# One flow for all attention: projection jobs of one bank beside every attention iteration

## The chip, the cores and the metric

The kernel runs on one core of one Trainium2 chip. The metric is the device time in microseconds (us), here the median of three runs. The core has a matrix engine (TensorE, PE in the profile, with its weight loads as PEld), VectorE (DVE), ScalarE (ACT), GpSimd (POOL) and the queue engine SyncE (SP). PE writes into a memory of eight banks of 128 rows by 512 fp32 columns.

## The reference

Two blocks of two layers each run one after the other on 512 tokens of width 1024. What matters here is where attention stands beside projections:

```python
def first_block(x, mem, ...):                    # twice
    a_in, b_x, b_b, b_c, q, k, v, gate_in = split_cols(rmsnorm(x) @ w_in[l], IN_SPLITS)
    br_a = multiscale_pool(a_in, pool_w[l], pool_scale[l]) @ w_branch_a[l]      # windows 2, 4, 8, 16
    br_b = (b_b * causal_dwconv(b_c * b_x, conv_b_w[l])) @ w_branch_b[l]
    br_c = dilated_attention(rope(q), rope(k), v) @ w_branch_c[l]               # 12 heads of 64
    x = x + rmsnorm((gates * branches).sum() @ w_out[l])
    x = x + rmsnorm(memory_cross_attention(rmsnorm(x), rmsnorm(mem), ...))      # 4 heads of 128, 256 keys
    x = x + rmsnorm(conv_swiglu(rmsnorm(x)))
def second_block(x, c, ctx, ...):
    # layer 0 ("AB"): window attention of 8 heads, and differential attention (two softmaxes) of 4
    # layer 1 ("C"): latent attention of 16 heads, queries and keys of 96, 768 keys, values of 64
```

## The kernel before

Every product is made of three matmuls in a split format (`mm3`, L452 to L454: high by high, low by high, high by low). A weight slab is 1024 rows by 128 columns. SP loads it into a ring of four, ACT casts its high part (`head`, L429), POOL makes its low part (`tail`, L436), and PE multiplies it with 512 token columns in 24 matmuls (`slab`, L456), or in 24 more of 256 columns where the 256 context tokens (T = 768) are in it too. PE's results go to two pairs of banks, `acc[0]` and `acc[1]`; transposed probabilities go to the pair `pt`, and there are two single banks, `ob[0]` and `ob[1]`.

An attention iteration is 128 queries of one head: scores on PE into an `acc` pair; the row maximum on DVE (L919, L1145 or L1138); the exponential on ACT (L895, L1085); six transposes on PE into `pt` (L862, L1033); a copy to the memory `sq` on ACT (L902, L1096); the product with the values on PE ("pv", L868, L1058); and on DVE a reciprocal and a scaling by it, here called the result (L942, L1164), which frees the bank that pv wrote.

- First block. In each of two layers four pool slabs and nine convolution slabs come first, with their DVE work (L2086 to L2120), then the mixing of the pool groups (L2135). Then twice (j = 0, 1) nine tiles of queries, keys and values (`pe_tiles`, L717; the rotary turn is a matmul with a permutation, L728) and eight attention iterations with no projection beside them (`pe_attention`, L844). Then the branch gates. The memory attention has twelve tiles and then sixteen iterations.
- Second block. `pe_stream` (L974) runs AB and C with parts of the next projection slabs beside the iterations. All scores of one iteration are in `acc[0]` (in AB's double iterations, those of the second map in `acc[1]`), and a tile of 768 columns takes the whole of `acc[1]`. The order in an iteration is scores, transposes, transposes of values, part of a tile, pv. The pv of iteration n writes `ob[n % 2]`. In C a head is four iterations, and its jobs are a query tile of 3 row groups and a key and value tile of 2.

The engines run their own programs and meet at semaphores; `dve_stream` (L1120) has in each iteration the maxima, the result of an earlier iteration, the end of the last tile and the start of the next.

Of the kernel before, what the change touches and what calls it, by code (L numbers as in the profile page):

```python
# [20 lines left out]
ALU = mybir.AluOpType  # L21
ACT = mybir.ActivationFunctionType
F32 = mybir.dt.float32
# [34 lines left out]
MH = 4  # L58
# [7 lines left out]
N_LOADS = 25  # L66
# [6 lines left out]
class Counts:  # L73
# [4 lines left out]
    def __init__(self):  # L78
        self.here, self.outer, self.narrow = {}, {}, False
# [12 lines left out]
    def turn(self, what):  # L92

        n = self.count(what)
        return 1 + n % 2 * 2 if self.narrow else n % 4
# [18 lines left out]
def two_blocks(nc, A, out):  # L114

    with ExitStack() as ctx:
# [25 lines left out]
        perm = keep("perm", [P, P])  # L142
# [29 lines left out]
        mask1 = z("mask1", [P, RES, TC], BF16)  # L172
# [3 lines left out]
        ql = z("ql", [P, 3, SEQ], F32R)  # L176
        kh = z("kh", [P, 3, SEQ], F32R)
        kl = z("kl", [P, 3, SEQ], F32R)
        vt = z("vt", [P, 3, RES, P])
        ot1 = z("ot1", [P, RES, P])  # L180
        z = Region(qkv_at, high)
        mgh = z("mgh", [P, KT, SEQ], F32R)
        mgl = z("mgl", [P, KT, SEQ], F32R)
        z = Region(qkv_at, high)
        ub = z("ub", [P, 2, PAD + SEQ])
        sa = z("sa", [P, 2, PAD + SEQ])
        poh = z("poh", [P, 4, SEQ], F32R)
        pol = z("pol", [P, 4, SEQ], F32R)
        zc = z("zc", [P, 2, PAD + SEQ])
        bxs = z("bxs", [P, 2, SEQ])  # L190
# [10 lines left out]
        ofl = z("ofl", [P, 4, SEQ], F32R)  # L201

# [37 lines left out]
        head_t = nc.alloc_sbuf_tensor_at("head_t", [P, SEQ], F32, offset=zone + 4 * TC)  # L240
        lat = z("lat", [P, 5, TC])
# [104 lines left out]
        s_sum, s_hi, s_raw, s_vt, s_ready = sem("s_sum"), sem("s_hi"), sem("s_raw"), sem("s_vt"), sem("s_ready")  # L346
        neg_ready = sem("neg_sink")
# [267 lines left out]
        def pe_linear_y(e, c, T, xh, xl, kt, ready, ada=(), flush=False):  # L615
            kts = [(k, k, P) for k in range(kt)]

            def body(e, i):
                for j in range(2):
                    slab(e, c, T, xh, xl, kts, fresh=1 if i + j == 0 else 0, ready=ready)  # L620
# [96 lines left out]
        def pe_tiles(e, c, tiles, kts, xh, xl, fresh=0, stats=False):  # L717

            take(e, c, acc_free + ([] if stats else [pt_free]) + ob_free)

            def post(j):
                t = tiles[j]
                e.wait_ge(raw_ready, c.next(raw_ready))
                if t["kind"] == "plain":
                    return
                if t["kind"] == "rope":
                    M = t["M"]
                    e.matmul(ob[j % 2][0:M, 0:SEQ], perm[0:M, 0:M], t2raw(j)[0:M, 0:SEQ], start=True,  # L728
                             stop=True).then_inc(post_done, 1)
                else:  # L730
                    n, r0 = t["n"], t["r0"]
                    past(e, pe_past)
                    for i, cols in enumerate(t["tok"]):
                        tr = e.transpose(pt[:, i * n // 512, i * n % 512:i * n % 512 + n],
                                         t2raw(j)[r0:r0 + n, cols], ident[r0:r0 + n, r0:r0 + n])
                    tr.then_inc(post_done, 1)

            out, last_v = 0, -1
            for j in range(len(tiles) + 1):
                if fresh and j == 0:  # L740
                    pe_wave(e, c, tiles[0]["T"], xh, xl, fresh=fresh, free=False, stats=stats)
                elif j < len(tiles) and not (fresh and j == 1):
                    t = tiles[j]
                    slab(e, c, t["T"], xh, xl, t.get("kts", kts), M=t["M"], free=False, c0=t.get("c0", 0))
                if j == 2 and stats:
                    take(e, c, [pt_free])
                if j:

                    if tiles[j - 1]["kind"] in ("v", "kv"):
                        need, last_v = last_v + 1, j - 1  # L750
                        if need > out:
                            e.wait_ge(tile_ready, c.next(tile_ready, need - out))
                            out = need
                    post(j - 1)
            e.wait_ge(tile_ready, c.next(tile_ready, len(tiles) - out))
            give(e, acc_free + [pt_free] + ob_free)

        def t2raw(j):
            return sq[:, j % 2, :]

        def act_tiles(e, c, tiles):

            N, at = len(tiles), []
            for j in range(N + 2):
                if j < N:
                    head(e, c)
                    at.append(c.turn("acc"))
                    done = c.next(slab_done)
                if 1 <= j <= N:
                    t = tiles[j - 1]  # L770
                    T, M = t["T"], t["M"]
                    if not t.get("rx"):
                        e.wait_ge(slab_done, done if j == N else done - 1)
                    need = c.next(tile_ready) if j >= 3 else 0
                    if not t.get("rx"):
                        if need:
                            e.wait_ge(tile_ready, need)
                        e.activation(v3(t2raw(j - 1)[0:M, 0:T], T), bank(at[j - 1], T, M), ACT.Copy)\
                         .then_inc(raw_ready, 1)
                if j >= 2 and tiles[j - 2]["kind"] != "v":  # L780
                    t = tiles[j - 2]
                    e.wait_ge(sum_ready, c.next(sum_ready))
                    e.activation(t["hi"], t.get("arrange", same)(t2[0:t["R"], j % 2, 0:t["T"]]), ACT.Copy)\
                     .then_inc(tile_hi, 1)
            c.next(tile_ready, min(2, N))

        def dve_tiles(e, c, tiles):

            for j in range(len(tiles) + 1):
                if j < len(tiles):  # L790
                    s, done = c.turn("slab"), c.next(slab_done)
                    if tiles[j].get("rx"):
                        e.wait_ge(slab_done, done)
                        e.tensor_tensor(t2raw(j)[:, 0:SEQ], one(s), rstd[:, 0:SEQ], ALU.mult).then_inc(raw_ready, 1)
                if j < len(tiles) and tiles[j]["kind"] != "v":
                    dve_sum(e, c, tiles[j], j)
                if j and tiles[j - 1]["kind"] != "v":
                    t = tiles[j - 1]
                    w = t2[0:t["R"], (j - 1) % 2, 0:t["T"]]
                    e.wait_ge(tile_hi, c.next(tile_hi))  # L800
                    e.tensor_tensor(t["lo"], t.get("arrange", same)(w), t["hi"].bitcast(F32), ALU.subtract)\
                     .then_inc(tile_ready, 1)
                if j < len(tiles) and tiles[j]["kind"] == "v":
                    e.wait_ge(raw_ready, c.next(raw_ready))
                    dve_values(e, c, tiles[j])
                    e.sem_inc(tile_ready, 1)

        def dve_sum(e, c, t, j):

            T, M = t["T"], t["M"]  # L810
            raw, w = t2raw(j), t2[0:t["R"], j % 2, :]
            e.wait_ge(raw_ready, c.next(raw_ready))
            if t["kind"] == "rope":
                turned_part = (ysum if t.get("rx") else (ysum, rstd)[j % 2])[0:M, 0:SEQ]
                e.tensor_tensor(w[:, 0:SEQ], raw[0:M, 0:SEQ], rope_c[0:M, :], ALU.mult).then_inc(dve_step, 1)
                if T > SEQ:
                    e.tensor_copy(w[:, SEQ:T], raw[0:M, SEQ:T]).then_inc(dve_step, 1)
                e.wait_ge(post_done, c.next(post_done))
                e.tensor_tensor(turned_part, ob[j % 2][0:M, 0:SEQ], rope_s[0:M, :], ALU.mult).then_inc(dve_step, 1)
                e.wait_ge(dve_step, c.next(dve_step, 3 if T > SEQ else 2))  # L820
                e.tensor_tensor(w[:, 0:SEQ], w[:, 0:SEQ], turned_part, ALU.add).then_inc(sum_ready, 1)
            else:
                e.tensor_copy(w[:, 0:T], raw[0:t["R"], 0:T]).then_inc(sum_ready, 1)
                if t["kind"] == "kv":
                    dve_values(e, c, t)

        def dve_values(e, c, t):

            e.wait_ge(post_done, c.next(post_done))
# [14 lines left out]
        def pe_attention(e, c, its):  # L844
            N = len(its)
            take(e, c, acc_free + [pt_free])
            for n in range(N + 2):
# [7 lines left out]
                if n >= 2:  # L855

                    e.wait_ge(pt_copied, c.next(pt_copied))
# [1495 lines left out]
```

## Time and profile before

| | |
|---|---|
| median of 3 runs | 4576.96 us (4574.52 to 4582.12) |
| the profiled execution | 4583.58 us, of which 4581.8 us span |
| PE busy | 91% of the span, mean granted clock 0.916 of full |
| DVE, ACT, POOL busy | 40%, 30%, 31% |

The profiled execution is one execution of the program; durations below come from it. The granted clock of TensorE has two levels, 2.4 GHz (1.00) and 1.2 GHz (0.50); a value between is a mean over time.

### The profile page before, as it was taken

How to read it: one execution, taken by the hardware profiler on the slowest of the kernel's cores; microseconds unless marked ns; L12 is line 12 of the kernel's file. 1: busy time of each engine (PE TensorE's matmuls, PEld its weight loads, DVE VectorE, ACT ScalarE, POOL GpSimd, SP SyncE). 2: the span in 40 equal slices, each digit the busy share in tenths (PEclk: the TensorE clock that was granted, in tenths of full speed). 3: DMA queues.
4: the chain of work that ended last, by engine and by line, in shares of the span. 5: the costliest groups of instructions: out<-in, count | busy, mean ns of one | idle time of the engine just before them, and what ended most of it. 6: DMA issues, size and time to landing. Idle time of an engine off the chain costs nothing.

```text
span 4581.8 us, 48460 instructions
## 1 busy us (share of the span) xinstructions
PE 4184.2 (91%) x19548; PEld 3461.2 (76%) x19548; DVE 1836.9 (40%) x3065; ACT 1392.0 (30%) x2044; POOL 1419.6 (31%) x644
## 2 busy tenths in 40 slices
PE   6899998999989999999988888889999879989998
PEld 4778767777668776767767777779999668876886
DVE  4433445654643243574454444341111544433113
ACT  3223334332322233433223333231111323343222
POOL 2213533655431254355541000112222200003442
PEclk9877999999997799999989988799999877789999
DMA  2211332444321133234431000012221100002332
GB/s 91 66 42 58 113 92 69 127 126 129 99 75 37 51 111 101 64 118 126 126 109 28 19 19 19 24 42 64 61 64 56 47 14 13 12 25 72 94 94 77
DMA packets 544827, 317.85 MB, mean 69 GB/s; under 512 B 35876, under 2 KB 517599, under 8 KB 544607
## 3 DMA queue, kind: packets, MB, share of 16 engines
q1 hardware_dynamic: 544335, 313.71, 23.4%
q8 instruction: 157, 2.57, 0.2%
q10 hardware_dynamic: 272, 1.05, 0.1%
q14 instruction: 63, 0.52, 0.0%
HBM read 312.62 MB, written 2.10 MB: 69 GB/s over the span
## 4 chain that ended last, share of the span: by engine, by line
PE 80%; DVE 12%; ACT 3%; issue 2%; POOL 1%; DMA 1%; SPq 0%; PEld 0%; DVEq 0%; PEldq 0%; ACTq 0%
PE acc L452 23%; PE acc L454 22%; PE acc L453 22%; PE ob L1058 3%; PE pt L1033 2%; PE ob L868 2%; PE ob L1310 2%; POOL wlo L436 1%; PE pt L862 1%; DVE small L1145 1%; DVE t L701 1%; DVE t L2169 1%; DVE t L592 1%; PE pt L688 1%; DVE hl L607 1%
## 5 line engine op out<-in xcount | busy, mean ns | idle before, releaser
L436 POOL TENSOR_TENSOR wlo<-wraw,whi 128x1024 fp32r<-128x1024 f32 (+5 forms) x640 | 1419.4, 2224 | 3126.6 <-ACT whi L429 3125.6
L452 PE MATMUL acc<-hh,whi 128*128 128x512 f32 (+4 forms) x3320 | 1297.6, 391 | 88.7 <-DVE hl L607 32.6
L454 PE MATMUL acc<-hh,wlo 128*128 128x512 f32 (+4 forms) x3320 | 1254.2, 378 | 0.0
L453 PE MATMUL acc<-hl,whi 128*128 128x512 f32 (+4 forms) x3320 | 1251.5, 377 | 0.0
L429 ACT ACTIVATE whi<-wraw 128x1024 fp32r<-128x1024 f32 (+5 forms) x640 | 625.0, 980 | 999.6 <-DMA wraw<-in_ada_w 269.0
L452 PEld LDWEIGHTS acc<-hh,whi 128*128 128x128 f32 (+1 forms) x3320 | 637.9, 192 | 243.2 <-issue 82.8
L453 PEld LDWEIGHTS acc<-hl,whi 128*128 128x128 f32 (+1 forms) x3320 | 638.3, 192 | 110.6 <-issue 17.9
L454 PEld LDWEIGHTS acc<-hh,wlo 128*128 128x128 f32 (+1 forms) x3320 | 636.1, 192 | 95.3 <-issue 0.2
L1439 DVE TENSOR_TENSOR t<-acc,sq 128x768 f32<-128x768 f32 (+1 forms) x44 | 36.3, 824 | 501.7 <-PE acc L454 501.7
L454 PE MATMUL acc<-act1h,wlo 128*128 128x512 f32 x528 | 209.5, 397 | 0.0
L1096 ACT ACTIVATE sq<-pt 128x768 f32<-128x768 f32 (+1 forms) x136 | 95.1, 699 | 375.2 <-PE pt L1033 375.1
L453 PE MATMUL acc<-act1l,whi 128*128 128x512 f32 x528 | 208.4, 395 | 0.0
L452 PE MATMUL acc<-act1h,whi 128*128 128x512 f32 x528 | 208.1, 394 | 0.0
L1145 DVE TENSOR_REDUCE small<-acc 128x1 f32<-128x768 f32 (+1 forms) x128 | 105.2, 822 | 245.0 <-PE acc L454 244.8
L653 DVE TENSOR_SCALAR y<-acc 128x512 f32<-128x512 f32 (+1 forms) x80 | 59.6, 745 | 353.1 <-PE acc L454 353.1
L655 DVE TENSOR_TENSOR y<-acc,y 128x512 f32<-128x512 f32 (+1 forms) x64 | 48.5, 758 | 282.0 <-PE acc L454 282.0
L1390 ACT ACTIVATE sq<-acc 128x768 f32<-128x768 f32 (+1 forms) x44 | 31.1, 706 | 389.3 <-PE acc L454 389.3
L1058 PEld LDWEIGHTS ob<-vc,sq 128*128 128x128 f32 x768 | 115.7, 230 | 21.2 <-ACT sq L1096 14.6
L1085 ACT ACTIVATE t<-acc,small 128x768 f32<-128x768 f32 (+1 forms) x128 | 101.0, 789 | 95.8 <-DVE small L1151 95.3
L562 DVE TENSOR_TENSOR zf<-acc,rstd 128x512 f32<-128x512 f32 x88 | 60.8, 691 | 170.5 <-PE acc L454 170.0
L1058 PE MATMUL ob<-vc,sq 128*128 128x64 f32 x768 | 116.5, 312 | 7.6 <-ACT sq L1096 7.6
L637 ACT ACTIVATE sq<-y 128x512 f32<-128x512 f32 (+1 forms) x70 | 47.3, 676 | 242.2 <-DVE y L653 154.2
(352 smaller groups left out, 6069.4 us busy)
## 6 DMA issues: line engine op xcount, KB each, us to landing
wraw<-in_ffn_w SPq DMA_DIRECT2D x120, 512.0 KB, 3.8
wraw<-in_w_in SPq DMA_DIRECT2D x102, 512.0 KB, 3.8
wraw<-in_ada_w SPq DMA_DIRECT2D x96, 512.0 KB, 4.0
wraw<-in_w_up SPq DMA_DIRECT2D x88, 512.0 KB, 4.0
wraw<-in_w_down SPq DMA_DIRECT2D x32, 512.0 KB, 4.3
wraw<-in_w_out SPq DMA_DIRECT2D x16, 512.0 KB, 4.0
wraw<-in_w_mkv SPq DMA_DIRECT2D x16, 512.0 KB, 4.0
wraw<-in_ab_w_in SPq DMA_DIRECT2D x14, 512.0 KB, 3.8
```

Source lines behind the costliest of these rows:

```text
L429: e.activation(whi[0:rows, s, a:b, 0:w], wraw[0:rows, s, a:b, 0:w], ACT.Copy).then_inc(hi_ready, 1)
L436: e.tensor_tensor(wlo[0:rows, s, a:b, 0:w], wraw[0:rows, s, a:b, 0:w], whi[0:rows, s, a:b, 0:w].bitcast(F32), ALU.subtract).then_inc(lo_re ...
L452: e.matmul(o, wh, xh, start=first, stop=False)
L453: e.matmul(o, wh, xl, start=False, stop=False)
L454: return e.matmul(o, wl, xh, start=False, stop=last)
L868: mm = e.matmul(ob[s][:, 0:t["dv"]], sq[:, s, j * P:j * P + P], vj, start=j == 0, stop=j == len(t["v"]) - 1)
L1033: tr = e.transpose(ptf[:, j * P:j * P + P], src[:, j * P:j * P + P], ident[:, :])
L1058: mm = e.matmul(ob[s][:, 0:p["dv"]], sq[:, 0, j * P:j * P + P], vj, start=j == 0, stop=j == len(p["v"]) - 1)
L1085: e.activation(t2[:, m, 0:w], src, ACT.Exp, bias=bias, scale=-1.0 if t["mask"] is not None else t["scale"], accum_out=small[:, den:den + 1 ...
L1096: e.activation(sq[:, 0, 0:w], ptf[:, 0:w], ACT.Copy).then_inc(s_copied, 1)
L1145: e.tensor_reduce(col(MX + n % 4), S, AX_X, ALU.max).then_inc(dve_step, 1)
L1310: mm = e.matmul(ob[1][0:4, :], sc4[:, k, :], rows[:, w, 4 * j:4 * j + 4, :].rearrange("p a m -> p (a m)"), start=k == 0 and rows is whi, s ...
```

## The change

The functions `pe_tiles`, `pe_attention` and `pe_stream`, and those of ACT and DVE that go with them, are replaced by one set, `pe_flow`, `act_flow` and `dve_flow`, for all attention:

- Scores of iteration n + 1 are made in tick n, in pair `acc[(n + 1) % 2]`, so that both pairs are for scores.
- All pv results go to `ob[0]`. A projection job is of one bank, `ob[1]`: tiles of 768 columns are two jobs, of 512 and 256. The order in a tick is scores (n + 1), transposes (n), pv (n - 1), then the job.
- In the first block each layer makes the nine head tiles (in `acc`) and then eight iterations with seven jobs beside them (four pool, three convolution), nine head tiles, and eight iterations with the six other convolution jobs. Mixing of pool groups comes after. The order of slab loads on SP follows.
- The memory attention has four tiles ahead, and eight tiles and four turns of its output (`feat`) beside its sixteen iterations.
- The rotary turn of the first block is a shuffle on DVE in place of the matmul with a permutation, whose constant is dropped.

```diff
-        def pe_stream(e, c, its, jobs, ticks, xh, xl):
...
-                if n:
-                    p, s = its[n - 1], (n - 1) % 2
-                    e.wait_ge(s_copied, c.at(s_copied, n))
-                    e.wait_ge(ob_free[s], c.next(ob_free[s]))
-                    for j, vj in enumerate(p["v"]):
-                        mm = e.matmul(ob[s][:, 0:p["dv"]], sq[:, 0, j * P:j * P + P], vj, start=j == 0,
-                                      stop=j == len(p["v"]) - 1)
-                    mm.then_inc(s_pv, 1)
...
+            for n in range(-1, max(N + 1, len(ticks))):
...
+                if n + 1 < N:
+                    ready(its[n + 1]["need"])
+                    scores(n + 1)
...
+                if 1 <= n <= N:
+                    t = its[n - 1]
+                    ready(t.get("need_v", t["need"]))
+                    e.wait_ge(s_copied, c.at(s_copied, n))
+                    e.wait_ge(ob_free[0], c.next(ob_free[0]))
+                    slot["pv"] = n
+                    for j, vj in enumerate(t["v"]):
+                        mm = e.matmul(ob[0][:, 0:t["dv"]], sq[:, 0, j * P:j * P + P], vj, start=j == 0,
+                                      stop=j == len(t["v"]) - 1)
+                    mm.then_inc(s_pv, 1)
+                if tick:
+                    part(tick)
...
+        def dve_flow(e, c, its, jobs, ticks, wide=False, extra=None):
...
+            for n in range(-1, max(N + 2, len(ticks))):
+                tick = ticks[n + 1] if n + 1 < len(ticks) else None
+                if n + 1 < N:
+                    for m in range(len(its[n + 1]["maps"])):
+                        maxima(n + 1, m)
+                if 0 <= n - 2 < N:
+                    result(n - 2)
+                if ends(before):
...
+                if ends(tick):
...
+                        e.wait_ge(*done)
+                        if j["kind"] == "rope":
+                            turned(j, s)
...
+                        elif j["kind"] == "pool":
+                            pooled(j, s)
+                        else:
+                            conv(j, s)
```

Here is PE in the stream of C, one iteration before. `kch` and `qch` are the high parts of keys and queries, `lath` that of the latents, `vc` the values.

```order
L452 MATMUL acc0<-kch_141,qch_145 128x512 [waits s_probs]
...
L1033 MATMUL pt<-ident_60,t2_67 128x128 [waits s_copied,s_probs]
L1033 MATMUL pt<-ident_60,t2_67 128x128 x5
L452 MATMUL acc1<-lath_139,whi_52 128x384 [waits acc_free3,acc_free1,slab_lo_ready]
...
L1058 MATMUL ob1<-vc_143,sq_68 128x64 [waits ob_free1,s_copied]
L1058 MATMUL ob1<-vc_143,sq_68 128x64 x5
```

And the same place of the change, PE in C, from the scores of one tick to the job of that tick:

```order
L459 MATMUL acc0<-kch_143,qch_147 128x512 [waits s_probs,s_ready]
...
L797 MATMUL ob1<-ident_59,sq_67 128x64 x3
L861 MATMUL pt<-ident_59,t2_66 128x128 [waits s_copied,s_probs]
L861 MATMUL pt<-ident_59,t2_66 128x128 x5
L872 MATMUL ob0<-vc_145,sq_67 128x64 [waits ob_free0,s_copied]
L872 MATMUL ob0<-vc_145,sq_67 128x64 x5
L459 MATMUL ob1<-lath_141,whi_52 128x256 [waits proj_free]
```

The pv of every iteration now waits for the one bank `ob0`, and stands ahead of the job instead of behind it.

On DVE, the same change in the stream of C: a result (L1006) of the change, the query job (L1033 to L1039), and the next tick's maximum (L990, L995) and result:

```order
L1006 TENSOR_SCALAR ot3_146<-ob0,small_62 128x64 [waits dve_step]
L1033 TENSOR_TENSOR head_w_137<-ob1,rope_c_56 96x512 [waits slab_done]
L1034 STREAM_SHUFFLE head_t_138<-ob1 96x512
L1038 TENSOR_TENSOR head_t_138<-head_t_138,rope_s_57 96x512 [waits dve_step]
L1039 TENSOR_TENSOR head_w_137<-head_w_137,head_t_138 96x512 [waits dve_step]
L990 TENSOR_REDUCE small_62<-acc1 128x1 [waits s_scores]
L995 TENSOR_SCALAR small_62<-small_62 128x1 [waits dve_step]
L1005 RECIPROCAL small_62<-small_62 128x1 [waits s_pv]
L1006 TENSOR_SCALAR ot3_146<-ob0,small_62 128x64 [waits dve_step]
```

Between the job and the freeing of `ob0` there are five instructions here; the order on DVE is as before, but then two banks took turns.

The first block of the change has on DVE the pool jobs at that place (this is the third, with three doublings), where before no attention ran beside them:

```order
L1043 TENSOR_TENSOR ub_87<-ob1,rstd_65 96x512 [waits slab_done,s_ready]
L1049 TENSOR_TENSOR sa_88<-ub_87 96x512 [waits dve_step]
L1049 TENSOR_TENSOR sa_88<-sa_88 96x512 [waits dve_step] x2
L1051 TENSOR_TENSOR mix_w_90<-sa_88,edge_60 96x16 [waits dve_step]
L1052 SCALAR_TENSOR_TENSOR mix_w_90<-sa_88,ub_87 96x496
L1055 TENSOR_TENSOR mix_w_90<-mix_w_90,ub_87 96x16 [waits dve_step]
L982 ISA t2_66,small_62<-acc1,mask1_81 128x768 [waits s_scores,s_tr]
```

The maximum of the next scores (L982), and behind it the result, follow the pool chain.

## Rows read from the trace of the kernel before

**Rows 1.** The page: busy time, share of the span, instructions, of each engine.

```profile
PE 4184.2 (91%) x19548; PEld 3461.2 (76%) x19548; DVE 1836.9 (40%) x3065; ACT 1392.0 (30%) x2044; POOL 1419.6 (31%) x644
```

**Rows 2.** Windows: first block, layer 0: pool and convolution, tiles, attention, sum of five.

Columns are start and end, length, busy time of PE, PEld, DVE, ACT and POOL with instructions, granted clock, share and rate of the DMA. The fourth and fifth stage, again tiles and attention, are left out and are in the sum.

```profile
54.70:158.60 103.90, 91.94 (x366) 67.57 (x365) 56.07 (x69) 33.28 (x44) 36.17 (x16) 0.94 0.23 68
158.60:214.10 55.50, 51.59 (x217) 39.69 (x215) 26.15 (x36) 14.27 (x13) 16.66 (x7) 1.00 0.29 85
214.10:272.60 58.50, 54.20 (x220) 49.53 (x221) 13.65 (x41) 16.63 (x27) 0.74 (x1) 0.50 0.00 1
...
sum 337.70, PE 311.84 PEld 252.96 DVE 134.58 ACT 92.47 POOL 74.19; mean PE 62.37 PEld 50.59 DVE 26.92 ACT 18.49 POOL 14.84
```

**Rows 3.** Windows: layer 1's mixing, memory attention, AB, C.

```profile
1213.30:1551.50 338.20, 313.52 (x1261) 253.92 (x1260) 142.41 (x234) 90.29 (x121) 74.18 (x32) 0.80 0.17 49
667.10:756.70 89.60, 80.10 (x471) 66.65 (x470) 54.18 (x109) 41.80 (x94) 27.04 (x12) 0.94 0.20 59
2462.50:2901.30 438.80, 372.14 (x2088) 330.49 (x2089) 207.71 (x650) 152.38 (x344) 37.37 (x15) 0.88 0.07 19
3728.90:4103.30 374.40, 338.77 (x1914) 299.06 (x1915) 159.84 (x368) 146.76 (x262) 24.54 (x28) 0.79 0.06 15
```

**Rows 4.** Windows: the two first pieces of a head of C; one round of AB.

```profile
3743.50:3753.40 9.90, 8.21 (x62) 7.33 (x60) 5.34 (x14) 6.70 (x13) 0.74 (x1) 1.00 0.04 13
3753.40:3763.60 10.20, 9.96 (x35) 8.47 (x36) 1.54 (x6) 2.02 (x4) 0.50 (x1) 0.50 0.01 2
...
2532.20:2644.80 112.60, 94.26 (x535) 84.03 (x535) 52.88 (x166) 38.42 (x86) 10.09 (x4) 0.89 0.07 19
```

**Rows 5.** Timeline of PE: gaps in C and in AB; in brackets the idle time.

```profile
3753.64 0.71 PE L452 MATMUL acc<-lath,whi 128*96 128x512 f32 x1 [1.93 <-DVEq L379]
...
2575.16 0.58 PE L452 MATMUL acc<-kdh,qdh 64*128 64x256 f32 x1 [4.16 <-ACT t L1085]
```

**Rows 6.** Timeline: an iteration of C with no job, full clock.

```profile
4065.02 0.47 PE L452 MATMUL acc<-kch,qch 96*128 96x512 f32 x1
...
4066.14 0.82 PE L1033 MATMUL pt<-ident,t 128*128 128x128 f32 x6
4066.34 0.96 DVE L1145 TENSOR_REDUCE small<-acc 128x1 f32<-128x768 f32 x1 [1.63 <-PE acc L454]
...
4067.59 0.28 DVE L1164 TENSOR_SCALAR ot<-ob,small 128x64 f32<-128x64 f32 x1
...
4067.86 1.55 PE L1058 MATMUL ob<-vc,sq 128*128 128x64 f32 x12 [0.90 <-ACT sq L1096]
```

**Rows 7.** Timeline: first block's pv at half clock, a memory iteration's maximum.

```profile
231.57 2.66 PE L868 MATMUL ob<-vt,sq 128*128 128x64 f32 x12
...
238.25 2.66 PE L868 MATMUL ob<-vt,sq 128*128 128x64 f32 x12
...
736.07 0.41 DVE L922 TENSOR_REDUCE small<-acc 128x1 f32<-128x256 f32 x1
```

**Rows 8.** Timeline of PE: matmul 2 and matmul 24 of one slab, full clock.

```profile
165.01 0.40 PE L453 MATMUL acc<-hl,whi 128*128 128x512 f32 x1
...
170.16 0.39 PE L454 MATMUL acc<-hh,wlo 128*128 128x512 f32 x1
```

**Rows 9.** Timeline of DVE: first and last of a pool, a convolution, a C query chain.

```profile
88.00 0.68 DVE L562 TENSOR_TENSOR ub<-acc,rstd 96x512 f32<-96x512 f32 x1
...
94.31 0.17 DVE L2093 TENSOR_TENSOR t<-t,ub 96x16 f32<-96x16 f32 x1
...
133.01 0.69 DVE L2111 TENSOR_TENSOR zc<-acc,bxs 128x512 f32<-128x512 f32 x1 [4.91 <-PE acc L454]
...
136.68 0.69 DVE L2117 TENSOR_TENSOR t<-t,rstd 128x512 f32<-128x512 f32 x1
...
3763.56 0.69 DVE L1194 TENSOR_TENSOR head_w<-acc,rope_c 96x512 f32<-96x512 f32 x1 [2.31 <-PE acc L454]
...
3765.76 0.69 DVE L1202 TENSOR_TENSOR head_w<-head_w,head_t 96x512 f32<-96x512 f32 x1
```

More of the change, by code:

```diff
@@ L712, in dve_postnorm @@
             e.wait_ge(x_ready, c.next(x_ready, 2))
[L717 to L806, printed above, removed]
@@ L1066, in pe_stream, with act_flow, exps @@
-            take(e, c, ob_free)
-            give(e, [acc_free[0], acc_free[2], pt_free] + ob_free + ([acc_free[1], acc_free[3]] if both else []))
-        def act_stream(e, c, its, jobs, ticks):
-            c.narrow = True
+        def act_flow(e, c, its, jobs, ticks, wide=False, extra=None):
             first, total = instances(its)
-            N, sums = len(its), 0
-            def exps(n, m):
-                t, i = its[n], first[n] + m
+            N, sums, raws, combs, dones, feats = len(its), 0, 0, 0, 0, 0
+            def exps(n):
+                t = its[n]
@@ L1088, in act_stream @@
             before = None
-            for n in range(N + 1):
-                t, tick = (its[n], ticks[n]) if n < N else (None, None)
-                if n:
+            for n in range(-1, max(N + 1, len(ticks))):
+                tick = ticks[n + 1] if n + 1 < len(ticks) else None
+                if 1 <= n <= N:
                     w = len(its[n - 1]["v"]) * P
@@ new lines, in act_flow @@
+                if n + 1 < N:
+                    exps(n + 1)
+                    combs += len(its[n + 1]["maps"]) == 2
+                if ends(before):
+                    j = jobs[before[0]]
+                    if j["kind"] in ("rope", "pool", "conv2") or j["kind"] == "plain" and j.get("rx"):
+                        sums += 1
+                        e.wait_ge(s_sum, c.at(s_sum, sums))
+                        e.activation(j["hi"], j.get("arrange", same)(j["work"][0:j["span"], 0:j["T"]]), ACT.Copy).then_inc(s_hi, 1)
@@ L1204, in dve_stream @@
-            before = None
-            for n in range(N + 2):
-                t, tick = (its[n], ticks[n]) if n < N else (None, None)
-                if t:
-                    maxima(n, 0)
-                if n >= 2:
+                M, T, w, u = j["M"], j["T"], j["work"], j["t"]
+                src = jbank(s)[0:M, 0:T]
+                if j.get("rx"):
+                    st(e.tensor_tensor(j["raw"][0:M, 0:T], src, rstd[0:M, 0:T], ALU.mult))
+                    jrelease(e, s)
+                    src = j["raw"][0:M, 0:T]
@@ L1645, in swap, with both @@
-        def swap(block, half):
-            return [p + half if p % block < half else p - half if p % block < 2 * half else p for p in range(32)]
+                         dst=otm[:, r, a * P:a * P + P], s=(r % 2,), need=needs[a][0], need_v=needs[a][1])
+                    for a in range(4) for r in range(4)]
+        all_tok = [slice(i * P, i * P + P) for i in range(4)]
+        def both(kind, hi, lo, **more):
+            return [dict(more, kind="rope", span=more["M"], T=SEQ, hi=hi[:, 0:SEQ], lo=lo[:, 0:SEQ], done=False),
+                    dict(more, kind="plain", span=more["M"], T=CTX, c0=SEQ, hi=hi[:, SEQ:TC], lo=lo[:, SEQ:TC], fetch=False)]
@@ L1669, in ticks_ab @@
-            return spread(72, groups)
+                for span, tiles in ((10, 3 if t == 0 else 2), (8, 2 if t < 3 else 0)):
+                    n = min(span, 6) if span == 8 else span
+                    for i in range(tiles):
+                        m = n * (i + 1) // tiles - n * i // tiles
+                        long = (2 * m + 1) // 3
+                        ticks += over(j, KT, long) + over(j + 1, KT, m - long)
+                        j += 2
+                    ticks += [None] * (span - (n if tiles else 0))
@@ L1671, in its_ab @@
+            return ticks
         def its_ab():
```

992 lines of the change are left out of this document (479 added, 513 removed).

## Prediction

> **What bounds the kernel now.** I read the busy shares first: PE is busy for 91% of the span and no other engine for more than 40% [rows 1]. So time can be saved where PE idles, or where it works at half clock. The windows by stage show where that is. In the first block, layer 0, pool and convolution slabs take 103.9 us at clock 0.94, nine tiles 55.5 us at 1.00, and eight attention iterations 58.5 us at 0.50; with the second round the stage takes 337.7 [rows 2], in layer 1 338.2 [rows 3]. PE is busy for 54 of the 58.5 us, so attention there waits little; it is slow because the clock is. Memory attention takes 89.6 us, AB 438.8 at clock 0.88, C 374.4 at 0.79 [rows 3]. One head of C is 23.9 us: 9.9 at full clock, 10.2 at half, 3.8 at full again [rows 4], and the half begins right behind an idle gap of 1.93 us [rows 5].
>
> The Trainium skill ("TensorE: Matmul & The Clock Gate", the section on HAM oscillation) says that waits between short stretches of matmuls can throw the clock back again and again, once in every step of a loop. The trace agrees for C: the gap of 1.93 us and the 10.2 us at half clock behind it come in every head.
>
> **The new wait.** Now pv of iteration n writes `ob[n % 2]`, so the result that frees a bank has a whole iteration's time. After the change all pv write `ob[0]`, ahead of the job. Within one tick PE makes the scores (n + 1) and transposes (n), and must then wait for result (n - 2), which on DVE stands behind the last job's chain and behind maxima (n + 1), which need the scores just made. The iteration of C without a job shows the price: the last transposes start at 4066.14 and pv could start about 0.58 later, at 4066.72 (my estimate: the six end 0.82 after their start, and pv's first weight load overlaps the last), but the maximum starts at 4066.34 and the result behind it ends at 4067.87 [rows 6], 1.53 us after. So PE idles 1.15 us in every tick, if DVE was free when the scores ended. In this iteration of before the gap of 0.90 is ACT's copy, in another place. Where a job's chain on DVE is longer than the scores, the rest is added: for the C query job the chain is 3763.56 to 3766.45, 2.9 us [rows 9], against 1.12 us of scores, and its tick's idle is about 3.05. Nothing covers these waits, as the job stands behind pv on PE's queue.
>
> **First block's mixing, per layer.** A slab of 512 columns is 24 matmuls, 0.234 us apart at full clock (5.15 us for 22 of them), 5.63 in all [rows 8]. 31 slabs are 174.5. Statistics of the first slab add 6.9 (my estimate from the first slabs' stretch). An attention iteration is 6.68 us at half clock with no gap [rows 7], so 3.34 at full, and 3.48 with its seams: 16 make 55.7. Turned values 3, features 1, mixing 2.8. PE's work is 244 us. Idle: after the third and fourth pool job (chains of 6.5 us for the fourth [rows 9], one pass less, 5.8, for the third) the wait is the chain, 0.2 for handing over and 1.53, less scores and transposes (1.54 and 0.58 of the 3.34 by my split): 5.4 and 6.1. After a convolution job with its three taps (4.4 us [rows 9]) it is 4.0, twice. The other 12 iterations idle 1.2, and starts and ends 6: 40 us together. After each of the four long idles I let one stretch of half clock follow, as long as that in C: 10.2 us, in which 5.1 us are lost [rows 4], 20 in all. 244 + 40 + 20 = 304 against 338 [rows 2, 3]: **-34 per layer, -68 for both**. Bounds: no half clock at all gives -54 per layer, half clock in all the attention ticks (their PE work, 55.7 and 13 slabs of 5.63, doubled, and half of the idle then covered) would give +55, and I take the value nearer the first because most of a tick is 5.6 us of dense slab, like the tiles now at 1.00.
>
> **The permutation matmul** leaves PE and becomes a shuffle on DVE. In the tile stage DVE is busy for 26 of 55.5 us [rows 2], and the new chain of a tile is some 4.6 us, under 5.63. It costs nothing; without that cover it would be the chain's excess, under 1 us per tile.
>
> **Memory attention.** Its maximum is of 256 columns and takes 0.41 [rows 7], so the chain from scores to result is about 1.2 us and the ticks without a job, or with a small one, lengthen by 0.65; 16 of them give **+10 per layer, +20 for both**. Lower bound: with PE busy 80.1 of 89.6 now [rows 3], even a perfect cover gives -9.
>
> **AB.** A round is 112.6 us at clock 0.89 with PE busy 94.3 [rows 4]. Clock 0.89 is half clock for 22% of it, 24.8 us, in which 12.4 are lost, so the work is about 81.9 at full clock; counted by the spacing of starts it is 79.4, which I take. New idle: 18 ticks by 1.15 (20.7), three rotary chains that outlast the scores by 1.9, five combinations of two maps by 1.0: 31 us, against 18 now. At full clock 110.4. If as much is lost to the clock as now, 122.8; if the clock is that of C now, some 130. The stage is 438.8/112.6 = 3.9 rounds: +40 to +68, **I take +50**; at full clock it would be -9.
>
> **C.** One head is four iterations, each 1.12 of scores (4065.02 to 4066.14), 0.58 of transposes and 1.36 of pv (1.55 less overlap) [rows 6], and 4.9 of jobs (9 matmuls of 512 columns for the query, 6 of 512 and 6 of 256 for keys and values at 0.234 and 0.12, and the turned values): 17.1. Idle 1.2 + 3.05 + 0.9 + 1.05 = 6.2: 23.2 at full clock, against 23.9 now. But the 3.05 stand where 1.93 now throws the clock to half for 10.2 us, which costs 5.1 [rows 4, 5]; some 1.1 of it comes back, since at half clock scores and transposes cover more of DVE's chain. 27.2 by head, +3.2, 14 heads: **+45**; bounds -12 (full clock) and +126 (half clock throughout: twice 17.1 less what hides, 33 by head). The last two heads, without jobs, keep 4.2 us per iteration.
>
> **The rest.** A key wait ahead of C's first scores goes (-6), and AB's first tiles are shorter (-3), both estimates: **-9**. SP's new order of loads moves the mask's load into the first tiles, where SP has slack.
>
> Sum: -68 + 20 + 50 + 45 - 9 = +38. The profiled execution is 4583.6, of which 4581.8 is span, and is 6.6 above the median of 4576.96. 4583.6 + 38 = 4621.6, less 6.6 is **4615 us** as a median.
>
> [...]
>
> **Rivals.**
> - *The clock holds in AB and C (chance 0.20).* The mechanism is the same wait, but PE's gaps are spread evenly, and the single gap that now precedes half clock is not reached. It decides whether a gap of 3.05 in C lowers the clock. Against it: 1.93 does now in each head; 4.16 in AB does [rows 5]. For it: in the iteration without a job a gap of 0.90 in every 4.2 us leaves full clock alone [rows 6]. -68 + 20 - 9 - 12 - 9 = -78: **4499**, on the other side.
> - *The bank's wait is mostly hidden (0.07).* DVE would have to free the bank earlier than its program says, or the clock gain be larger: with half of each idle and full clock, the first block gives 2 x (264 - 338) = -148, AB 3.9 x (95 - 112.6) = -69, C 14 x (20.1 - 23.9) = -53: with -9, **4298**.
> - *Half clock through all of C (0.20).* The mechanism: a gap of 1.15 in each tick, beside the 3.05, keeps the clock from rising again once it has fallen. Against it: it rises again in each head now [rows 4]. +126 in place of +45: **4696**; if AB goes too, more.
> - My forecast: 0.50. Left over: 0.03 for cases outside.
>
> **How the numbers follow.** The range takes in my forecast, the first rival and the third: 4490 to 4710. Within it AB's bounds (-10 to +18 about my value) are covered. A measurement of this kernel tells 0.2% (9 us) from no change. Faster: 0.20 + 0.07 + 0.04 of my own case's low side = 0.31; same 0.07; slower 0.62.
>
> **What would show it.** In the profile after: gaps of PE ahead of pv (L872) released by DVE's result or its queue in nearly every tick, about 1.15 us in C's ticks and 3.0 behind a query job, 4 to 6 behind pool jobs; a first-block mixing of about 304 us with clock above 0.85; a head of C of 27 us with clock below 0.8; an AB of 490. The prediction is wrong if those gaps are absent, if the clock in C is above 0.9 (then 4500), or if the first block stays at half clock.

## The result and the profile after

The changed kernel takes 4680.03 us (median of 4 runs, 4670.82 to 4688.98), the kernel before 4579.34 (4 runs, 4574.52 to 4582.12). The ratio is 1.0221, 95% interval 1.0195 to 1.0246: slower by 100.7 us. Forecast were 4615, +38. The time is in the range and on the side that was given, but the change costs over twice what the sum said.

The page of the changed kernel, its busy shares and the clock of 40 slices (the shares of before are in [rows 1]):

```profile
span 4672.6 us, 48668 instructions
PE 4146.5 (89%) x19562; PEld 3372.9 (72%) x19562; DVE 1828.3 (39%) x3076; ACT 1393.1 (30%) x2082; POOL 1420.8 (30%) x644
PEclk9798999999989899999988878899999888989999
```

PE is busy for less time than before (4146.5 us against 4184.2) at a higher mean clock (0.929 against 0.916), and the span is 91 us longer. So PE waits more: it idles for 526 us in place of 398. The view of PE's waits says for what: engine, line, what was waited for, us in total, times, longest.

```profile
PE ob L872 <- DVE ot L1006: 178.1, 123, 3.8
PE acc L459 <- POOL wlo L443: 34.8, 48, 1.7
...
PE ob L872 <- DVE otm L1006: 28.3, 28, 1.6
PE ob L872 <- DVEq L1009: 26.7, 22, 3.2
```

L872 is the pv, L1006 the result, and L1009 the release of the bank behind a result of AB's double iterations: 233 us in 173 waits. In the kernel before pv never waits for a result. The idle time grew by only 129 us, so about 100 us of other waits went. The wait for a slab's low part (L443 above) was shorter before:

```profile
PE acc L452 <- POOL wlo L436: 14.8, 29, 2.4
```

One head of C in the changed kernel, the timeline with the idle time in brackets:

```profile
3807.83 0.82 PE L861 MATMUL pt<-ident,t 128*128 128x128 f32 x6
...
3809.20 0.69 DVE L1039 TENSOR_TENSOR head_w<-head_w,head_t 96x512 f32<-96x512 f32 x1
3809.81 0.95 DVE L990 TENSOR_REDUCE small<-acc 128x1 f32<-128x768 f32 x1
...
3811.05 0.28 DVE L1006 TENSOR_SCALAR ot<-ob,small 128x64 f32<-128x64 f32 x1
3811.49 1.52 PE L872 MATMUL ob<-vc,sq 128*128 128x64 f32 x12 [2.83 <-DVE ot L1006]
...
3832.77 0.82 PE L861 MATMUL pt<-ident,t 128*128 128x128 f32 x6
```

This is the wait that the prediction worked out: PE has ended the transposes and could start pv; DVE ends the query's chain (L1039), takes the maximum (L990), then the result (L1006), and only then does pv start. This head takes 24.94 us, from 3807.83 to 3832.77; others are longer, as shown further down.

By stages: before (first fence) and after (second), cut at the same events (first block's mixing in two layers, memory attention in two, AB, C; each with the work between it and the stages beside it). The columns are as in [rows 2].

```profile
44.60:404.70 360.10, 329.71 (x1325) 265.75 (x1326) 140.03 (x226) 105.57 (x140) 78.99 (x34) 0.81 0.17 50
1205.90:1564.20 358.30, 329.16 (x1313) 264.95 (x1312) 151.24 (x250) 99.38 (x131) 78.95 (x34) 0.80 0.17 50
659.80:756.70 96.90, 82.99 (x476) 67.68 (x475) 58.05 (x115) 46.00 (x100) 27.04 (x12) 0.93 0.21 60
1826.40:1927.50 101.10, 85.95 (x478) 70.36 (x476) 59.02 (x115) 45.82 (x100) 26.84 (x12) 0.90 0.20 58
2376.60:2996.50 619.90, 504.10 (x2727) 447.22 (x2726) 276.76 (x785) 200.28 (x406) 63.80 (x26) 0.86 0.09 24
3595.70:4112.50 516.80, 435.06 (x2270) 368.81 (x2268) 239.03 (x494) 190.15 (x327) 39.37 (x38) 0.78 0.06 17
```

```profile
44.80:394.50 349.70, 308.29 (x1336) 242.20 (x1337) 145.09 (x234) 103.32 (x140) 75.42 (x33) 0.87 0.17 49
1219.50:1555.60 336.10, 294.35 (x1325) 231.46 (x1324) 156.16 (x259) 96.99 (x131) 75.47 (x33) 0.90 0.18 51
653.80:768.90 115.10, 86.50 (x477) 68.55 (x475) 45.77 (x109) 46.42 (x98) 26.79 (x12) 0.92 0.17 51
1817.30:1932.50 115.20, 85.56 (x478) 67.44 (x476) 45.74 (x108) 46.33 (x98) 26.74 (x12) 0.94 0.17 51
2383.30:3070.10 686.80, 531.18 (x2724) 438.99 (x2723) 279.64 (x759) 201.24 (x422) 61.92 (x26) 0.82 0.08 22
3669.20:4204.70 535.50, 417.19 (x2264) 342.68 (x2262) 240.05 (x530) 194.94 (x357) 38.93 (x38) 0.86 0.06 17
```

A clock of 0.87 over 349.7 us is half clock for 2 x 0.13 of it, 91 us. The table has this for each stage, beside the lengths in three of the experiments below (same cuts). "Forecast" and "measured" are the change of a stage's length. All are us.

| stage | before | after | forecast | measured | half clock, before and after | result first | job first | both |
|---|---|---|---|---|---|---|---|---|
| mixing, two layers | 718.4 | 685.8 | -68 | -33 | 280, 158 | 641.6 | 627.3 | 601.7 |
| memory attention, two | 198.0 | 230.3 | +20 | +32 | 34, 32 | 210.6 | 205.7 | 202.2 |
| AB | 619.9 | 686.8 | +50 | +67 | 174, 247 | 602.7 | 573.6 | 563.9 |
| C with its start | 516.8 | 535.5 | +36 | +19 | 227, 150 | 462.1 | 507.0 | 451.8 |

What lies outside these stages is 5.5 us longer together, which the forecast had at nothing.

### The profile page after: what moved, and what is told of

It reads as the page before. It is cut to its first block and busy times, and to the rows that moved or that the text cites. A ratio compares the mean times of both kernels' runs of the same rounds, so it can differ in the third digit from the quotient of the medians.

```text
span 4672.6 us, 48668 instructions
## 1 busy us (share of the span) xinstructions
PE 4146.5 (89%) x19562; PEld 3372.9 (72%) x19562; DVE 1828.3 (39%) x3076; ACT 1393.1 (30%) x2082; POOL 1420.8 (30%) x644
## 3 DMA queue, kind: packets, MB, share of 16 engines
q10 hardware_dynamic: 272, 1.05, 0.1%
## 5 line engine op out<-in xcount | busy, mean ns | idle before, releaser
L443 POOL TENSOR_TENSOR wlo<-wraw,whi 128x1024 fp32r<-128x1024 f32 (+5 forms) x640 | 1420.6, 2226 | 3216.4 <-ACT whi L436 3215.6
L459 PE MATMUL acc<-hh,whi 128*128 128x512 f32 (+2 forms) x2744 | 1074.5, 392 | 71.7 <-POOL wlo L443 33.7
L461 PE MATMUL acc<-hh,wlo 128*128 128x512 f32 (+2 forms) x2744 | 1042.2, 380 | 0.0
L460 PE MATMUL acc<-hl,whi 128*128 128x512 f32 (+2 forms) x2744 | 1039.9, 379 | 0.0
L459 PEld LDWEIGHTS acc<-hh,whi 128*128 128x128 f32 x2744 | 524.2, 191 | 212.4 <-POOL wlo L443 55.7
L460 PEld LDWEIGHTS acc<-hl,whi 128*128 128x128 f32 x2744 | 524.2, 191 | 91.7 <-issue 11.8
L461 PEld LDWEIGHTS acc<-hh,wlo 128*128 128x128 f32 x2744 | 523.6, 191 | 86.5
L459 PE MATMUL ob<-hh,whi 128*128 128x512 f32 (+2 forms) x576 | 239.7, 416 | 1.0 <-DVEq L764 1.0
L990 DVE TENSOR_REDUCE small<-acc 128x1 f32<-128x768 f32 (+1 forms) x160 | 118.7, 742 | 303.8 <-PE acc L461 299.9
L460 PE MATMUL ob<-hl,whi 128*128 128x512 f32 (+2 forms) x576 | 227.2, 394 | 0.0
L461 PE MATMUL ob<-hh,wlo 128*128 128x512 f32 (+2 forms) x576 | 225.2, 391 | 0.0
L920 ACT ACTIVATE sq<-pt 128x768 f32<-128x768 f32 (+3 forms) x200 | 132.3, 661 | 137.6 <-PE ob L872 137.5
L872 PE MATMUL ob<-vc,sq 128*128 128x64 f32 x768 | 109.8, 299 | 69.4 <-DVE ot L1006 68.4
L872 PEld LDWEIGHTS ob<-vc,sq 128*128 128x128 f32 x768 | 102.3, 212 | 82.2 <-issue 81.0
```

The lines of the kernel that those rows point to most:

```text
L443: e.tensor_tensor(wlo[0:rows, s, a:b, 0:w], wraw[0:rows, s, a:b, 0:w], whi[0:rows, s, a:b, 0:w].bitcast(F32), ALU.subtract).then_inc(lo_re ...
L459: e.matmul(o, wh, xh, start=first, stop=False)
L460: e.matmul(o, wh, xl, start=False, stop=False)
L461: return e.matmul(o, wl, xh, start=False, stop=last)
L872: mm = e.matmul(ob[0][:, 0:t["dv"]], sq[:, 0, j * P:j * P + P], vj, start=j == 0, stop=j == len(t["v"]) - 1)
L920: e.activation(sq[:, 0, 0:w], ptf[:, 0:w], ACT.Copy).then_inc(s_copied, 1)
```

## The experiments

### Result ahead of maxima

In `dve_flow` of the changed kernel:

```diff
+                if 0 <= n - 2 < N:
+                    result(n - 2)
                 if n + 1 < N:
                     for m in range(len(its[n + 1]["maps"])):
                         maxima(n + 1, m)
-                if 0 <= n - 2 < N:
-                    result(n - 2)
```

> DVE takes the result (n - 2) ahead of the maxima (n + 1); nothing else is changed. Theory (the pv on PE waits because the result stands behind maxima that need the scores of the same tick): of the 233 us that pv waits for the result in the changed kernel, the part that every tick pays (about 1.15 us) goes, and only what a job's chain outlasts scores and transposes stays (about 1.7 us in C's query ticks, 2 to 4 behind pool and convolution jobs). Some 60 to 80 us of wait are left, the time falls by 130 to 180 us, to 4500 to 4550. Rival (the wait moves: maxima come later by a result, 0.45 us, so exponentials and transposes are late instead): gaps ahead of the transposes take the place, the time falls by less than 50.

Measured: 4461.07 us (4458.24 to 4462.0), ratio to before 0.9747 (0.9731 to 0.9764), 219 under the changed kernel. PE's waits:

```profile
PE ob L872 <- DVE ot L1006: 68.8, 38, 2.8
...
PE ob L872 <- DVE otm L1006: 12.6, 16, 1.1
...
PE ob L872 <- DVEq L1009: 8.7, 7, 2.1
```

90 us are left of 233, where 60 to 80 were expected, and the transposes wait no more than in the changed kernel (24.4 us against 23.9). The cause given by the theory holds and its rival falls, but the time is 39 us under the low end of the expectation. The gain is larger than the 143 us of wait that went: the mean clock rose from 0.929 to 0.943.

### Job ahead of pv

In `pe_flow`, `part(tick)` is moved ahead of the pv, nothing else:

```diff
+                if tick:
+                    part(tick)
                 if 1 <= n <= N:
                     t = its[n - 1]
...
                     mm.then_inc(s_pv, 1)
-                if tick:
-                    part(tick)
```

> PE makes the job of a tick ahead of the pv; the single bank and DVE's order stay. Theory: the job (0.75 to 5.6 us) covers the wait for the result, so the gap stays only in ticks without a job (the ends, two of eighteen ticks in a round of AB, some of memory attention) and behind short jobs: 30 to 60 of 233 us are left, 4470 to 4520. Rival (DVE is late by its own load in AB and C, so that the wait is only moved to the next scores or transposes): the time falls by less than 60.

Measured: 4445.78 us (4443.74 to 4446.94), ratio to before 0.9713 (0.9698 to 0.9727), 234 under the changed kernel. The pv waits for 34 us in all, 42 times, as expected; the time is 24 us under the low end of the expectation. But another wait grew, that of a job for its own bank, which DVE frees:

```profile
PE ob L459 <- DVEq L764: 45.3, 37, 1.9
...
PE ob L874 <- DVE ot L1006: 16.7, 24, 1.6
PE ob L874 <- DVEq L1009: 11.5, 10, 1.7
...
PE ob L874 <- DVE otm L1006: 5.9, 8, 1.2
```

So part of the rival is true in C, where 31 of these 45 us lie. C takes 507.0 us where result first has 462.1, but that is not the wait: PE idles there for 81 us in this kernel and for 80 in the other. The clock makes the whole difference, 0.83 in C against 0.90.

### Both

> Both edits together. Theory: almost no wait for the result is left (under 20 us), and what remains of idle time is of other kinds; 4440 to 4490, a little under either alone, as each removes most of the same wait. If they added up fully (each its own wait) it would be 4350 or below. Rival (PE's work and clock are the bound once most of the gaps are closed): the three kernels lie within 20 us of each other.

Measured: 4361.91 us (4360.43 to 4365.65), ratio to before 0.9531 (0.9517 to 0.9545). That is 318 under the changed kernel, where each edit alone gave 219 and 234: they overlap, but by less than I expected, and the time is 78 under the low end of mine. Only 9 us of pv waiting for a result are left (3.8, 2.9 and 2.7 in the three rows).

224 us of this wait went, but other waits grew, and PE's idle time fell by 171 us (526 to 355). PE's busy time fell by 138 (4146.5 to 4008.3) with the same 19562 matmuls: that part is the clock, 0.956 over the span. The window of C:

```profile
3444.60:3896.30 451.70, 381.03 (x2262) 314.45 (x2261) 244.31 (x530) 195.08 (x357) 39.02 (x38) 0.92 0.07 20
```

### The dense head tiles

ACT casts a slab ahead of the last tile's high part, and DVE makes the low part of a query or key tile after the next tile's turn, so that its work buffer alternates:

```diff
+                early = wide and ends(tick) and jobs[tick[0]]["kind"] != "feat" and jobs[tick[0]].get("done", True)
+                if early:
+                    head(e, c)
...
+                late = wide and ends(before) and jobs[before[0]]["kind"] == "rope"
+                if not late:
+                    lows(before)
...
+                if late:
+                    lows(before)
...
-                            work=t2[:, 0, :], t=t2[:, 1, :], swap=swap(HD, 8))
+                            work=mix_w[:, g % 2, :], t=t2[:, 1, :], swap=swap(HD, 8))
```

> Only the dense head tiles of the first block: ACT casts the next slab ahead of the last tile's high part, and DVE makes the low part of a tile behind the next tile's turn, in another buffer. Theory (the loop of DVE turn, ACT high part, ACT cast of the slab, GpSimd low part and PE slab sets 7.23 us per tile, where PE needs 5.63): tiles take 5.7 to 6.0 us, 24 tiles of queries and keys in two layers give 25 to 35 us, 4645 to 4655. Rival (DVE itself is full with its chain, 1.95 us for the product that meets GpSimd's work): the period stays above 6.8, and less than 12 us are won.

Measured: 4670.57 us (4657.12 to 4676.11), ratio to before 1.0200 (1.0179 to 1.0222), 9.5 under the changed kernel, whose interval (1.0195 to 1.0246) overlaps this one: the medians alone do not show a gain. First one tile of the changed kernel; the PE gap is 1.36 us and the next slab starts 7.23 us after:

```profile
93.52 0.69 DVE L1030 TENSOR_TENSOR sq<-acc,rstd 128x512 f32<-128x512 f32 x1
94.35 1.95 DVE L1033 TENSOR_TENSOR t<-sq,rope_c 128x512 f32<-128x512 f32 x1
...
98.45 1.13 ACT L932 ACTIVATE kh<-t 128x512 fp32r<-128x512 f32 x1 [5.14 <-DVE t L1039]
99.49 1.05 ACT L436 ACTIVATE whi<-wraw 128x1024 fp32r<-128x1024 f32 x1
...
100.61 2.37 POOL L443 TENSOR_TENSOR wlo<-wraw,whi 128x1024 fp32r<-128x1024 f32 x1 [4.86 <-ACT whi L436]
...
103.03 0.50 PE L459 MATMUL acc<-hh,whi 128*128 128x512 f32 x1 [1.36 <-POOL wlo L443]
110.26 0.50 PE L459 MATMUL acc<-hh,whi 128*128 128x512 f32 x1 [1.36 <-POOL wlo L443]
```

And in the experiment DVE, the first instruction of two tiles and one between:

```profile
96.08 0.69 DVE L1034 TENSOR_TENSOR sq<-acc,rstd 128x512 f32<-128x512 f32 x1
...
98.32 2.10 DVE L1042 TENSOR_TENSOR t<-t,rope_s 128x512 f32<-128x512 f32 x1
...
102.18 0.69 DVE L1034 TENSOR_TENSOR sq<-acc,rstd 128x512 f32<-128x512 f32 x1
```

The loop of five steps was the limit: with two of them moved, 7.23 us of DVE's period became 6.10, PE has no gap ahead of the slabs between 89 and 103 us, and its waits for low parts fell from 34.8 to 14.7 us. DVE is now without a gap between 96.08 and 102.18; one product takes 2.1 us there and not 0.69, and it began while GpSimd made a low part. DVE's period is longer than PE's slab, so it falls behind, and PE waits for it once at the end of these tiles (1.24 us at 109.01). So both the theory and its rival have a part: the period lies between theirs, and the time misses the 4645 to 4655 of the theory. In the two profiled executions the mixing stages are 16 us shorter, and AB, whose code is the same, is 13 us longer (700.1 against 686.8); see the last section.

### All three edits

> Result first, job first, and the order of the dense tiles, together. Theory (the tiles' loop and the wait for the result are separate places, so their gains add): the kernel with result first and job first (4361.9) less what the tiles gained in their own stages, 16 us: 4340 to 4352. Rival (the tile edit's 10 us were given back by the clock in later stages, as AB took 13 us more there with the same code): within 5 us of 4362.

Measured: 4335.8 us (4332.86 to 4349.14), ratio to before 0.9494 (0.9471 to 0.9517). It is 26 under the kernel with two edits (17 by the ratios to before), 4 under the low end of the expectation, and the fastest of all. So the gain of the tile edit comes on top of that of the other two, and the rival (within 5 us) falls.

### A delay ahead of each result

In the changed kernel, ahead of each result on DVE:

```diff
                 e.wait_ge(s_pv, c.at(s_pv, n + 1))
+                for _ in range(3):
+                    st(e.tensor_copy(col(60), col(63)))
```

> The changed kernel with three copies of one column put ahead of every result on DVE, 0.2 us each with their waits, 0.6 in all, 200 times: 120 us of DVE time. Theory (each result sits on the path from scores to pv, in nearly every tick): nearly all of it shows in the time, and the longer gaps cost some clock too: +90 to +160, 4770 to 4840. Rival (the gaps ahead of pv are PE's time lost to half clock and to other queues, DVE has slack since it is busy for 39%): less than +40.

Measured: 4908.27 us (4895.19 to 4918.05), ratio to before 1.0748 (1.0721 to 1.0776): +228 against the changed kernel, with a delay of 0.55 us (a group of three takes 0.52 and the reciprocal follows at once), 110 us for 200 results. PE's waits, and behind them C's window:

```profile
PE ob L872 <- DVE ot L1008: 244.7, 134, 4.4
PE ob L872 <- DVE otm L1008: 43.4, 28, 2.2
PE ob L872 <- DVEq L1011: 40.2, 22, 3.7
```

```profile
3787.80:4425.40 637.60, 495.36 (x2264) 407.32 (x2262) 269.60 (x722) 195.07 (x357) 38.86 (x38) 0.74 0.05 14
```

The waits rose from 233 to 328 us, 95 of the 110. So nearly every result is on the path, as the theory says. But the time rose by more than twice that: PE idles for 92 us more and is busy for 129 us more (4275.5) with the same matmuls, at a mean clock of 0.899. In C alone it is +102 us, for 64 delays of 0.55 (35 us), and the clock there is 0.74 in place of 0.86: 332 us at half clock in place of 150. The expectation's top was too low by 68 since it gave the clock too little.

### The same delay, covered

> The same 120 us of DVE copies in the kernel with result first and job first. Theory (there the result has slack behind scores, transposes and job): under a third shows, +10 to +40, 4372 to 4402, most of it in the memory attention and in the ticks without a job. Rival (DVE is by now the bound in the attention stages): +90 or more, as in the kernel without the two edits.

Measured: 4454.10 us (4443.65 to 4467.73), ratio to before 0.9749 (0.9721 to 0.9777): +92 over the kernel with two edits, where the same delay cost 228 in the other. The expectation of +10 to +40 failed, and the size is the one that the rival named. PE idles for 41 us more than in the kernel with two edits, and is busy for 37 us more. The largest part of the idle time is pv waiting for results again, 28 us in place of 9; waits for the bank of a job rose by 6 us, and those of the transposes for ACT's copy by as much (to 38.8). The waits, and behind them C's window:

```profile
PE ob L459 <- DVEq L764: 35.3, 31, 1.9
...
PE ob L874 <- DVE ot L1008: 13.4, 20, 1.8
...
PE ob L874 <- DVE otm L1008: 7.3, 10, 1.3
PE ob L874 <- DVEq L1011: 7.2, 10, 1.2
```

```profile
3476.60:3974.00 497.40, 415.33 (x2264) 344.60 (x2262) 274.28 (x722) 194.82 (x357) 38.96 (x38) 0.85 0.07 18
```

DVE is busy for 274 of 497 us in C, so it is not full, and the rival's mechanism does not hold as it was put. So the two edits cover the delay only in part: 19 of 110 us come back as waits for a result, where 95 did without them. C alone has half of the loss (451.8 to 497.4) and its clock fell from 0.92 to 0.85. Half clock rose from 72 to 149 us there, which is worth up to 38 of the 46 us. What made the clock fall, with gaps of at most 1.9 us in the waits shown, is not settled by this run.

### One bank in the kernel before

In `pe_stream` and `dve_stream` of the kernel before the bank index is 0 for every iteration:

```diff
-                    p, s = its[n - 1], (n - 1) % 2
+                    p, s = its[n - 1], 0
...
-                t, s = its[n], n % 2
+                t, s = its[n], 0
```

> The kernel before, with one edit: in the streams of AB and C all pv results go to the first output bank, so a pv waits for the result of the iteration just before it, as in the change. Its pv stays behind the part of a tile, its attention in the first block stays with two banks. Theory (the single bank costs only together with the place of pv ahead of the job and the result behind the maxima): transposes, part and the copy that pv waits for anyway cover 1.5 to 2.5 us, which is all that maxima and result take, so the time stays within 20 us of before. Rival (one bank in place of two is by itself what costs): AB and C lose as in the change, +60 or more.

Measured: 4581.39 us (10 runs) against 4576.74 (13 runs), ratio 1.0016 (1.0005 to 1.0027). In time, one bank costs 5 us in AB and C where pv stands behind a part of a tile, and the rival falls. But the bank is not free of waits in that order. The view of PE's waits has a row that the kernel before has not:

```profile
PE ob L1058 <- DVE ot L1164: 32.5, 36, 3.4
```

In AB and C of the changed kernel the same wait is 169 us. The 32.5 do not show in the time because the mean clock is higher (0.923 against 0.916; between 3740 and 4050 us, in C, 0.89 against 0.79): PE idles for 20 us more and is busy for 25 us less. So most of the cost comes from the order around the single bank; that the rest was made good by the clock is luck as far as these runs show.

## Why the prediction was right or wrong

**The new wait: right in its place, about a quarter too large.** Forecast were gaps ahead of pv in C of 3.05 us behind the query job, and 0.9, 1.05 and 1.2. Measured are 2.83, 0.60, 0.34 and 1.06. Behind the third and fourth pool job 5.4 and 6.1 were forecast, and 3.29 and 3.80 came; behind two convolution jobs 4.0 each, and 2.91 and 3.00 came. By stage the forecast had 68 us in mixing, 20 in memory attention, 121 in AB and 87 in C, 296 in all; measured are 36, 28, 101 and 68, the 233 us. Result first and job first each take most of it away, and the delay adds to it by 95 of 110 us.

**The step that failed is the clock behind the wait, as a term of the sum.** In the mixing stages I let a stretch of 10.2 us of half clock follow each of four long idles of a layer, and none follow the short ones: 41 us of half clock, 20 us lost. Measured are 91 and 67 us, up to 45 and 33 lost. The idle time was right: PE idles for 41.4 and 41.7 us in these windows, 4.5 of which lie in the 20 to 22 us that they have beyond the stage of the forecast, and 40 were forecast. So the clock has by itself about the 35 us by which the stage missed. The longest stretch at half clock stands behind a short gap, and the same gap did nothing 37 us earlier:

```profile
322.25 1.52 PE L872 MATMUL ob<-tails,sq 128*128 128x64 f32 x12 [0.92 <-DVE ot L1006]
...
359.12 2.79 PE L872 MATMUL ob<-tails,sq 128*128 128x64 f32 x12 [0.92 <-DVE ot L1006]
```

```profile
359.00:382.90 23.90, 21.56 (x82) 18.62 (x83) 4.11 (x12) 6.30 (x10) 2.35 (x1) 0.50 0.00 1
```

In AB my +50 was 51 us of idle time, 10 less of work, and 10 more lost to the clock than now (2.6 a round). Measured is +67: 40 of idle time, and half clock up from 174 to 247 us, up to 37 lost in place of 10.

In C the same term erred the other way. Thirteen heads of the changed kernel (first line, from one query gap to the last) and twelve of the kernel before (second):

```profile
3811.49:4149.61 338.12, 273.11 (x1599) 232.65 (x1600) 138.28 (x338) 128.73 (x248) 21.35 (x26) 0.88 0.06 15
3753.64:4040.42 286.78, 263.69 (x1476) 233.41 (x1477) 126.02 (x288) 113.01 (x204) 18.26 (x24) 0.79 0.06 15
```

A head takes 26.0 us, where 27.2 were forecast and 23.9 were needed before. It idles for 5.0 (6.2 forecast) and is at half clock for 6.2 (10.2 forecast, and 10.0 before), though its longest gap has grown from 1.93 to 2.83 us. That took C from the forecast +36 to +19.

What the runs put in the place of a fixed stretch behind each long gap is a price and not a rule. Between the changed kernel and its variants the matmuls are the same, and PE's busy time moved with its idle time: -127 us of idle time and -89 of busy time (result first), -147 and -83 (job first), -171 and -138 (both), +92 and +129 (the delay), +41 and +37 (the delay on top of both). Idle time that was added or taken away thus cost between 0.6 and 1.4 times its length once more. It does not hold for the tile edit (-19 and +2), nor from the kernel before to the changed one or to the one with a single bank: there the idle time rose and the mean clock rose too. Nor does it hold for every stage alone: C has the same idle time with result first and with job first, 45 us apart. What makes the clock fall behind one gap and not behind an equal one stays open.

**"It costs nothing" was wrong** for the turn that went from PE to DVE in the dense tiles. I compared DVE's chain of 4.6 us with PE's 5.63. The chain is not alone: ACT's high part, DVE's low part (1.1 us), the cast of the next slab and GpSimd's low part stand behind it in one loop of 7.23 us; a tile before, its permutation matmuls included, took 6.47 (the permutations of two tiles start at 163.92 and 170.39 in the trace of before). Also, one of the products took 1.95 us, not 0.69. The trace has 19 us of PE waiting for the low part in the two mixing stages of the changed kernel. It was luck that the idle time came out right as a whole: the waits for a result there were 32 us under the forecast.

**Memory attention** was +32 and not +20: pv waits for 28 us in it, and I had priced 0.65 us a tick where 28 waits are 1.0 on average.

**The rivals.** "The clock holds in AB and C" did not come: in AB the clock fell from 0.86 to 0.82, and in C it rose, but to 0.86 only. "Half clock through all of C" did not come either, though its 4696 is near the time; that nearness is chance. The mechanism of 4298, a wait that is mostly hidden, does not exist in the changed kernel, but the two edits made it: 4362, and 4336 with the third. That the time lies inside the range is in part luck too: mixing, AB and memory attention missed upwards by 64 us together, and C downwards by 17.

## What to carry to other kernels

When a buffer that alternated becomes a single one, look at what stands between its release and its next use on both engines. Here it cost 5 us of time in one order and 233 us of waiting in another, and two moved pieces of code turned 2.2% slower than before into 4.7% faster. Free a buffer before you start on work that waits for the engine you are blocking, and put long independent work between two steps that hand a buffer back and forth. Work that is moved off the other engine's path is covered in part only: the delay still cost 92 us with both edits. When an operation goes to a less busy engine, follow the whole loop through all engines to the next item, not that engine's own chain.

## What the runs showed of the hardware

- Idle time of PE that was added cost more than its length. In the changed kernel 110 us of delay ahead of the results made 95 us of waiting and 228 us of time, with the mean clock from 0.929 to 0.899. The Trainium skill ("TensorE: Matmul & The Clock Gate", the section on HAM oscillation) describes such a clock that falls again and again with waits in a loop; these runs agree and give its price here.
- A gap of a given length does not decide alone. Gaps of 2.83 us in C went with 6.2 us of half clock in a head, the single one of 1.93 before [rows 5] with 10.0. Behind gaps of 0.92 us the clock stayed full in one place and was at half for 23.9 us in another. C took 462 us with result first and 507 with job first, with 80 and 81 us of idle time, and clocks of 0.90 and 0.83.
- The same code in AB took 686.8 us in one profiled execution and 700.1 in another, of a kernel that differs only in the first block, with clock 0.82 and 0.80. Executions of one and the same kernel differ by as much (4670.8 to 4689.0 for the changed one), so these two do not say whether the edit had a part in it, and a comparison by stages of single executions needs a margin of this size.
- A product of two fp32 operands of 128x512 on DVE took 0.69 us, and 1.95 to 2.10 where it began while GpSimd made a slab's low part. One whose first operand lies in a bank of PE (`sq<-acc,rstd`) took 0.69 there too: at 93.52 us, within GpSimd's instruction of 93.39 to 95.76, ahead of the product of 1.95 at 94.35.
